# Attention openings of ten fillings in two groups, shorter late fillings, and a sum of squares moved behind the second maxima product

## The reference

```python
s = einsum('bhqd,bhkd->bhqk', qb, kh) * scale + cb[..., :, None] - c[..., None, :]
s = where(key_pos[None, :] <= q_pos[:, None], s, -inf)
o = einsum('bhqk,bhkd->bhqd', softmax(s), vh)          # 8 heads of 64, blocks of 128 queries
y_b = rmsnorm(o, on_w) * silu(zh)
g_a, g_b = split(sigmoid(h @ W_gates + gate_b), 2)      # 1024 columns each
merged = g_a * (y_a @ w_up_gdn) + g_b * (y_b @ w_up_fox)
out = rmsnorm(x + merged @ w_out)
```

## Time and profile before

| | us |
|---|---|
| median of 3 runs | 968.0 |
| lowest and highest run | 963.97, 968.58 |
| the profiled execution, its own time | 967.72 |
| its span | 965.9 |
| attention, first maxima product of pair 0 to the end of pair 3 | 487.8 to 739 |
| PE busy in the span | 934.1 (97%) |
| DVE busy, ACT busy | 611.2 (63%), 446.5 (46%) |

### The profile page before, as it was taken

One profiled execution on the slowest core, in us unless ns is written; L12 is line 12 of the kernel. 1 busy time (PEld: TensorE's weight loads), 2 busy tenths in 40 slices (PEclk: granted clock), 3 DMA queues, 4 the chain that ended last, 5 costly groups with the idle time before them and its releaser, 6 DMA issues.

```text
span 965.9 us, 16052 instructions
## 1 busy us (share of the span) xinstructions
PE 934.1 (97%) x6484; PEld 702.7 (73%) x6484; DVE 611.2 (63%) x981; ACT 446.5 (46%) x778; POOL 19.7 (2%) x28
## 2 busy tenths in 40 slices
PE   4999999999999999999989999999999999999997
PEld 3778787788888876766765665665666888888885
DVE  7387568799999824464476786785773434246252
ACT  7465654533433414532646636456354533334131
POOL 1000002020000000000000000000000000000000
PEclk9999999999999999999999999999999999999999
DMA  8111351249223482322453325225123331223162
GB/s 249 40 45 47 94 174 47 68 156 215 89 89 103 138 244 74 100 67 78 138 178 103 110 98 152 80 97 156 34 66 120 121 110 58 85 109 110 28 199 79
DMA packets 115745, 104.89 MB, mean 109 GB/s; under 512 B 34192, under 2 KB 95760, under 8 KB 115288
## 3 DMA queue, kind: packets, MB, share of 16 engines
q1 hardware_dynamic: 104008, 80.27, 29.8%
q10 hardware_dynamic: 10512, 19.40, 5.5%
q0 software_dynamic: 1152, 4.19, 1.3%
HBM read 76.84 MB, written 27.00 MB: 108 GB/s over the span
## 4 chain that ended last, share of the span: by engine, by line
PE 44%; DVE 4%; ACT 2%; issue 1%; DVEq 0%; ACTq 0%
PE pj L2117 6%; PE pj L2119 5%; PE pj L2118 5%; PE pc L2248 3%; PE pa L2216 3%; PE pa L2185 1%; PE pj L2128 1%; PE pj L2130 1%; PE pj L2129 1%; DVE qk L1849 1%; PE pb L2263 1%; DVE pa L1899 1%; PE pc L2384 1%; PE pc L2383 1%; PE pb L2384 1%
## 5 line engine op out<-in xcount | busy, mean ns | idle before, releaser
L144 PE MATMUL pj<-h_hi,w_hi 128*128 128x512 f32 x504 | 204.2, 405 | 1.4 <-ACT xc L641 0.9
L145 PE MATMUL pj<-h_lo,w_hi 128*128 128x512 f32 x504 | 197.4, 392 | 0.0
L146 PE MATMUL pj<-h_hi,w_lo 128*128 128x512 f32 x504 | 197.1, 391 | 0.0
L144 PEld LDWEIGHTS pj<-h_hi,w_hi 128*128 128x128 f32 x504 | 94.8, 188 | 25.0 <-issue 2.4
L146 PEld LDWEIGHTS pj<-h_hi,w_lo 128*128 128x128 f32 x504 | 94.9, 188 | 20.4
L145 PEld LDWEIGHTS pj<-h_lo,w_hi 128*128 128x128 f32 x504 | 95.0, 188 | 18.0 <-issue 0.2
L2117 PE MATMUL pj<-h_hi,w_hi 128*128 128x512 f32 x248 | 103.2, 416 | 0.3 <-PEq L315 0.3
L2119 PE MATMUL pj<-h_hi,w_lo 128*128 128x512 f32 x248 | 97.0, 391 | 0.0
L2118 PE MATMUL pj<-h_lo,w_hi 128*128 128x512 f32 x248 | 96.8, 390 | 0.0
L641 ACT ACTIVATE xc<-pj 128x512 f32<-128x512 f32 x40 | 24.0, 600 | 108.3 <-PE pj L146 107.8
L2117 PEld LDWEIGHTS pj<-h_hi,w_hi 128*128 128x128 f32 x248 | 46.5, 188 | 22.0 <-issue 12.9
(11 more groups left out here) (355 smaller groups left out, 1840.2 us busy)
## 6 DMA issues: line engine op xcount, KB each, us to landing
w_raw<-in_w_in SPq DMA_DIRECT2D x48, 512.0 KB, 4.4
fox_scratch<-xc ACTq DMA_DIRECT2D x40, 256.0 KB, 2.8
qkv<-in_x SPq DMA_DIRECT2D x8, 512.0 KB, 6.5
fa<-rows_scratch POOLq DMA_DIRECT2D x8, 512.0 KB, 5.0
rv<-fr_scratch SPq DMA_DIRECT2D x16, 256.0 KB, 4.0
ma<-m_scratch SPq DMA_DIRECT2D x8, 512.0 KB, 4.1
rv<-in_w_out SPq DMA_DIRECT2D x8, 512.0 KB, 3.7
w_raw<-in_x SPq DMA_DIRECT2D x8, 512.0 KB, 4.5
```

What stands on the lines that cost most here:

```text
L144: nc.tensor.matmul(o, w_hi[:, slot, k], h_hi[:, k, cols], start=(k == 0), stop=False)
L145: nc.tensor.matmul(o, w_hi[:, slot, k], h_lo[:, k, cols], start=False, stop=False)
L146: last = nc.tensor.matmul(o, w_lo[:, slot, k], h_hi[:, k, cols], start=False, stop=(k == KT - 1))
```

## The change

`FILLS` gives the openings of pairs 0, 2 and 3 ten fillings instead of eight (pair 1 keeps eight), and takes six away from late steps: one each from steps 10 and 12 of pair 0, one from step 12 of pair 1, two from step 12 of pair 2, one from step 12 of pair 3. An opening's fillings stand in two groups (three, and the rest) instead of three (two, one, five). `square_sums` of the pair before stands behind `max_scores(p, 7)` instead of ahead of the filling before it.

```diff
-        FILLS = ((8,) + (4,) * 4 + (0, 4) * 4) * PAIRS + (5, 4, 4, 3)
+        FILLS = ((10,) + (4,) * 4 + (0, 4, 0, 4, 0, 3, 0, 3)
+                 + (8,) + (4,) * 4 + (0, 4, 0, 4, 0, 4, 0, 3)
+                 + (10,) + (4,) * 4 + (0, 4, 0, 4, 0, 4, 0, 2)
+                 + (10,) + (4,) * 4 + (0, 4, 0, 4, 0, 4, 0, 3) + (5, 4, 4, 3))
...
                     max_scores(p, 0)
                     max_scores(p, 1)
-                    fill(2)
+                    fill(3)
                     max_scores(p, 2)
                     turn_values(p, 0)
-                    fill(1)
                     max_scores(p, 3)
-                    fill(5)
+                    fill(FILLS[PER * p] - 3)
                     turn_max(p, 0)
                     for v in range(4):
                         max_scores(p, 4 + 2 * v)
...
                             turn_values(p, 1)
                         else:
                             values(p, v - 1)
+                        fill(1)
+                        max_scores(p, 5 + 2 * v)
                         if v == 1 and p:
                             square_sums(p - 1, 1)
-                        fill(1)
-                        max_scores(p, 5 + 2 * v)
                         fill(3)
                     turn_max(p, 1)
...
                         if v == 8:
                             square_sums(p, 0)
-                        fill(4)
+                        fill(FILLS[PER * p + v + 2])
```

## The result

| | us | runs |
|---|---|---|
| before, median (lowest to highest) | 967.56 (963.97 to 968.58) | 4 |
| changed, median (lowest to highest) | 976.25 (971.91 to 978.32) | 4 |
| ratio, with its 95% interval | 1.0085 (1.0063 to 1.0107) | |
| profiled execution of the changed kernel, its span | 971.91, 970.1 | |

The change makes the kernel 8.7 us slower: 976.25 us, where 974.7 was forecast.

The account below looks back on a forecast made before the run. PE was taken to bound the kernel. The terms -3.2 + 3.2 + 3.75 + 0.85 gave +4.6 us, +7.0 with the clock, so 974.7 us; the range of 8 in 10 was 968.5 to 977.0.

Parts of the forecast that it names:

- openings of 10, hidden under DVE: Openings of pairs 0, 2 and 3: six more fillings cost nothing under DVE's reductions, saving 4.1 us elsewhere, 3.2 after losses.
- end of pair 0 gives one filling back: Last scores of pair 0: PE already waits there, so one removed filling only lengthens the wait; 0.69 us of gain lost.
- end of pair 3: Last two values products of pair 3: one filling less makes PE wait for the exponential of slot 11; 0.26 us lost.
- wait of unit 3: Pair 0, step 1: the first up product now comes ahead of `gated` of unit 2, and PE waits; +3.2 us.
- wait of unit 13: Pair 3, step 1: the first up product now comes ahead of `gated` of unit 12, and PE waits; +3.75 us.
- sum of squares in pair 2: Pair 2: `max_scores` 7 can't start earlier, so the moved sum of squares comes on top; +0.85 us.
- clock: PE's clock falls to half behind each of the two new waits, in pairs 0 and 3; +2.4 us together.
- The rival that the waits cost nothing: `gated` of units 2 and 12 ends before PE needs it: -2.4 us, 965.4, chance 0.07; only one wait, another 0.10.
- the rival with DVE as the new bound: DVE, held back at `max_scores` 6, lengthens a later PE wait by 1 to 3 us: 976 to 978, chance 0.10.
- I take 1.2 for each: Clock loss behind each new wait, taken between bounds of nothing and 1.6 us, nearer to the upper.
- the wait of 1.79 us: A PE wait in the DeltaNet part, followed by 3.5 us at mean PEclk 0.53; taken as evidence for the clock loss.
- The rival with the clock at full speed: Both waits come, but the clock stays up or falls once: +4.6 to +5.8 us, 972.3 to 973.5, chance 0.33.

Follow-up runs that it names:

- exp. 1: Kernel before with only the sum of squares moved behind the second maxima product: 968.41 us, ratio 1.0006 (0.9994 to 1.0019).
- exp. 6: Changed kernel with 8 and 15 extra unused PE products in the two waits of pairs 0 and 3: 972.65 us, ratio 1.0063 against the kernel before.
- exp. 5: The changed kernel itself run once more for its trace, nothing edited: 976.13 us, ratio 1.0097 (1.0081 to 1.0112) against the kernel before.
- experiment 7: Changed kernel with `gated` ahead of `split_w_lo` and `split_up_lo` in DVE's steps: 972.53 us, ratio 1.0059 against the kernel before.
- experiment 4: Changed kernel with fillings set so that neither pair 0 nor pair 3 has its wait, sum of squares still moved: 967.55 us, ratio 0.9997.
- experiments 2 to 4: Changed kernel with fillings set to remove the wait of pair 0, of pair 3, and both: 972.57, 971.64 and 967.55 us.
- experiment 2: Changed kernel with pair 0's fillings as before the change, so without the wait of pair 0: 972.57 us, ratio 1.0050 against the kernel before.
- experiment 10: Changed kernel with the sum of squares back in its old place, ahead of the filling: 974.14 us, ratio 1.0067 against the kernel before.

## Why the prediction was right, step by step

| term | forecast | measured | where |
|---|---|---|---|
| openings of 10, hidden under DVE | waits gone | 1.3 us left of 5.3, pair 1 only | waits after |
| end of pair 0 gives one filling back | 0.69 | 0.70 | starts, below |
| end of pair 3 | 0.26 | 0.39 | starts, below |
| wait of unit 3 | 3.2 | 2.94 idle, 3.11 late | timeline |
| wait of unit 13 | 3.75 | 3.50 idle, 3.66 late | timeline |
| sum of squares in pair 2 | 0.85 | 0.90, and 0.89 alone | exp. 1 |
| clock | 2.4 | 3.15 and 4.5 in two traces, 3.5 timed | below, exp. 6 |
| whole | +7.0 | +8.7, +9.2 | result, exp. 5 |

**The openings** were read rightly: DVE's reductions set their end, and six fillings under them cost nothing. **The ends** give back what they were charged, and a little more. The idle times there (0.16 and 0.62 us in pair 0, 0.17 in pair 3) show only part of it, because the trace counts them from the end of the last product, latency included; the distances between starts show all. In pair 0, from the second `turn_max` to the first maxima product of pair 1 it was 550.78 - 519.48 = 31.30 us before and is 551.74 - 521.12 = 30.62: two fillings less should save 1.38 and save 0.68, so 0.70 is lost. In pair 3, from the last values products to the next filling, it was 737.25 - 736.45 = 0.80 us and is 741.40 - 740.21 = 1.19: 0.39 lost, where 0.26 was forecast.

**The two waits** hold to 0.1 us, with their causes: in pair 0 DVE's row of work up to `gated` (experiment 7 takes part of it away and PE waits that much less), in pair 3 the walk from `plus` over ACT to `gated` (DVE idle for 1.36 us, as in the earlier trace rows). (Late is against the place of before, moved with the pair's first `turn_max`: 501.47 - 3.11 = 498.36 in pair 0, where `turn_max` comes 3.11 earlier, and 690.81 - 0.80 = 690.01 in pair 3.) Taking both away takes the loss away (experiment 4). PE did not get the time back within the pair, and DVE did not become a new bound: apart from the named waits, PE's waits in the attention are those of before. The rival that the waits cost nothing is out, by experiments 2 to 4. The time alone couldn't tell the forecast from the rival with DVE as the new bound: 976.25 lies above the narrow 973.6 to 975.8 and inside that rival's 976 to 978. The traces decide between them: the two pairs grow by their waits and the lost clock, and on the way from each pair to the next nothing grows (table below).

**The sum of squares** cost what the distance of pair 1 said.

**The clock** is the term that was mis-sized. The step "I take 1.2 for each" had the mechanism right and the size low: a stretch of 3.4 us at PEclk 0.50 holds 1.7 us less work if PE is busy all through, and in pair 0 it was, since it begins 0.9 us behind the end of the wait and not within it. That is 1.8 us of busy time more. In pair 3 it starts 0.16 us inside the wait, and the clock was down for a second stretch in three of the five traces that have this wait (experiments 2, 5 and 7). What a pair lost beyond its wait was 4.75 - 3.11 = 1.64 us in pair 0 and 5.17 - 3.66 = 1.51 in pair 3 in the first trace, 3.15 together; in experiment 5 pair 3 lost 2.84, which makes 4.5. Experiment 6 gives 3.5 us for both in the timed runs, 1.1 more than forecast. The support that the prediction took from the wait of 1.79 us was also weaker than one trace could tell: a wait of 1.8 us stands in that place in all twelve traces, and a slow stretch follows it in nine. The rival with the clock at full speed (972.3 to 973.5) is where the kernel of experiment 6 came out, with the waits and without slow stretches: 972.65.

The Trainium skill, page "TensorE: Matmul & The Clock Gate", section "HAM oscillation — how this bites in real kernels", says that a wait between bursts of matmuls puts PE back to the half clock, so that the next burst starts slow. Experiment 6 agrees: with products in the waits, whose result nobody reads, PEclk stays at 1.00 and the kernel is 3.5 us faster.

The sum can be made again from the stretches between the pairs' `turn_max` in the changed kernel's first trace:

| stretch | before | after | difference |
|---|---|---|---|
| pair 0, first to second `turn_max` | 22.22 | 26.97 | +4.75 |
| on to pair 1 | 40.44 | 39.77 | -0.67 |
| pair 1, first to second | 23.14 | 23.20 | +0.06 |
| on to pair 2 | 40.10 | 38.69 | -1.41 |
| pair 2, first to second | 23.35 | 24.25 | +0.90 |
| on to pair 3 | 39.38 | 38.06 | -1.32 |
| pair 3, first to second | 23.12 | 28.29 | +5.17 |
| on to the first product of `w_out`'s stage | 161.40 | 161.20 | -0.20 |
| sum | 373.15 | 380.43 | +7.28 |

The rows "on to" hold what the openings give. 0.72 of the 1.41 is a wait that moves by itself (last section); without it they come to 2.9 us, where 3.2 was forecast. So the +7.0 is near the +7.3 of this trace partly by luck: the clock was 0.75 us dearer than forecast and the openings gave 0.35 less, and the wait that went by itself hid 0.72 of that. The second slow stretch, 1.3 us in experiment 5, brings the trace near the 8.7 of the timed runs. How often it comes there no trace shows.

## What to carry to other kernels

Filler work that is numbered through has a second meaning: two more pieces under one stall move every later piece, and a piece that waits for another engine may come ahead of what it waits for. List the first product of each unit with the instruction that it waits for, before and after, and put their times side by side. In this kernel waits of 2.94 and 3.50 us on the densest engine had to be charged twice: for themselves, and for the slow clock behind them, 1.5 to 2.8 us more each.

## What the runs showed of the hardware

- **The clock and the length of a wait.** 1.2 to 1.4 us of idle time, with full products behind, never took PE's clock down in the attention, in any of the twelve traces. 2.94 us did in all four traces that have it and 3.50 us in all five. With products in the same two waits (experiment 6) the clock stayed at 1.00.
- **The clock stays down for different times behind the same wait.** Behind the 3.50 us of pair 3 it was 3.4 us in two traces (the first of the changed kernel, experiment 10) and 6.8 us in three (experiments 2, 5, 7):

```profile
691.50:698.30 6.80, 5.35 (x21) 3.24 (x21) 2.10 (x5) 2.39 (x5) 0.00 (x0) 0.50 0.22 84
```

  This is experiment 7, where the wait ends at 692.95, so the clock fell 1.45 us ahead of its end. In the other two with 6.8 us it fell 0.53 us (experiment 2) and 0.65 us (experiment 5) ahead of it. In the two with 3.4 us it fell 0.16 us ahead of it (693.51 and 693.67) and 0.21 us behind it (experiment 10). So in these five traces the clock stayed down longer where it fell well inside the wait. No run was made to test this.
- **The start of the kernel varies.** A slow stretch near 20 us is missing in one of the twelve traces and is 3.4 us long in four, 6.8 in five and 10.2 in two; one near 355 us is there in nine. The first `turn_max` comes at 494.15 us in one trace and at 498.50 in another, with nothing changed ahead of the attention. A single profiled execution can therefore hide or feign 4 us: the comparison has to be made over a stretch with the same events at both ends.
- **One wait moves by itself.** The sum of squares waits for DVE's `add_squares`, which stands behind a pass over norm rows that come back by a transfer. In pair 1, DVE before:

```profile
600.50 1.28 DVE L1840 SCALAR_TENSOR_TENSOR tmp<-tmp,vecs,rv 128x1024 f32<-128x1024 f32 x1 [2.65 <-DMA rv<-fr_scratch]
601.70 0.69 DVE L1930 TENSOR_TENSOR usq<-usq,fac 128x512 f32<-128x512 f32 x1
```

PE waited 0.7 us for it before, and not at all after, although no edit touches it; over the attention these waits add up to 0.5 us in experiment 1, 0.9 in experiment 2, 1.3 in experiment 4, 1.2 in experiment 7 and 2.2 in experiment 6. Why the transfer lands at different times was not tried. It blurs differences under 1 us, and up to 2 us between single traces.
